# Six sums over partitions as two rounded products instead of one full-precision product

## The reference

```python
# state-space branch, after the gate: norm over 1024 channels
y = y.reshape(b, s, SSD_INNER) * jax.nn.silu(z.astype(jnp.float32))
return rmsnorm(y, norm_w).astype(z.dtype)
...
# retention branch: norm over the 256 channels of each of 4 heads
y = y * lax.rsqrt(jnp.mean(y * y, axis=-1, keepdims=True) + EPS)
y = y.reshape(b, s, RET_WIDTH) * jax.nn.silu(g.astype(jnp.float32))
...
# latent queries: norm over Q_LORA_RANK = 384 channels
c_q, q_mem = jnp.split(h @ w_in, [Q_LORA_RANK], axis=-1)
q = (rms_norm(c_q, g_q_lora) @ w_uq).reshape(b, s, MLA_HEADS, QK_HEAD_DIM)
```

## Time and profile before

| | |
|---|---|
| median of 3 runs | 2901.81 us (2900.05 to 2902.97) |
| the profiled execution | 2900.07 us, of which the span of the trace is 2898.2 us |
| granted TensorE clock | 1.0 of full speed, all through |
| TensorE busy | 2877.2 us |
| VectorE busy | 2192.0 us |
| ScalarE busy | 1383.4 us |
| GpSimd busy | 397.5 us |

### The profile page before, as it was taken

The page is one execution under the profiler, slowest core; times in us unless marked ns, Lnnn a source line. Parts: engine busy times, 40 slices in busy tenths (PEclk is TensorE's granted clock), DMA queues, the critical chain, the costliest instruction groups (busy, mean ns, idle before and its releaser), DMA issues.

```text
span 2898.2 us, 49038 instructions
## 1 busy us (share of the span) xinstructions
PE 2877.2 (99%) x17524; PEld 2531.7 (87%) x17524; DVE 2192.0 (76%) x3578; ACT 1383.4 (48%) x2252; POOL 397.5 (14%) x320
## 2 busy tenths in 40 slices
PE   9999999999999999999999999999999999999999
PEld 7888788778999888999887899989999887699987
DVE  8797574667999868888566888848889767688862
ACT  4653732344655525555233655525555236465541
POOL 0043250001111001110033011001110021011100
PEclk9999999999999999999999999999999999999999
DMA  3222123225577326773334477436773332257723
GB/s 139 102 92 91 66 95 116 73 80 179 160 183 180 89 95 181 181 180 103 107 109 132 129 180 180 117 114 179 184 182 106 107 111 74 83 155 184 182 80 109
DMA packets 144003, 375.93 MB, mean 130 GB/s; under 512 B 16176, under 2 KB 16432, under 8 KB 143472
## 3 DMA queue, kind: packets, MB, share of 16 engines
q1 hardware_dynamic: 110448, 309.44, 31.3%
q0 software_dynamic: 33408, 64.50, 13.0%
HBM read 371.78 MB, written 2.10 MB: 129 GB/s over the span
## 4 chain that ended last, share of the span: by engine, by line
PE 92%; DVE 5%; ACT 1%; issue 1%; DMA 0%; POOL 0%; SPq 0%; DVEq 0%; ACTq 0%; POOLq 0%
PE ps L1038 17%; PE ps L1040 17%; PE ps L1039 17%; PE ps L1492 12%; PE ps L1494 12%; PE ps L1493 12%; PE ps L1435 1%; DVE region_low L3594 0%; PE ps L1718 0%; PE ps L1755 0%; PE ps L1210 0%; DVE w_lo L2652 0%; DVE region_low L3222 0%; PE ps L1199 0%; PE ps L1424 0%
## 5 line engine op out<-in xcount | busy, mean ns | idle before, releaser
L1829 ACT ACTIVATE w_hi<-raw 128x1024 fp32r<-128x1024 f32 x300 | 315.8, 1055 | 281.4 <-DMA raw<-in_wstream 281.3
L1492 PE MATMUL ps<-h_hi,w_hi 128*128 128x256 f32 x1440 | 409.6, 284 | 1.6 <-DVE stage L3441 0.6
L1493 PE MATMUL ps<-h_lo,w_hi 128*128 128x256 f32 x1440 | 407.4, 283 | 0.0
L1038 PE MATMUL ps<-h_hi,w_hi 128*128 128x512 f32 (+1 forms) x883 | 347.4, 393 | 2.6 <-DVE w_lo L2652 1.8
L1040 PE MATMUL ps<-h_hi,w_lo 128*128 128x512 f32 (+1 forms) x883 | 340.7, 386 | 0.0
L1039 PE MATMUL ps<-h_lo,w_hi 128*128 128x512 f32 (+1 forms) x883 | 340.5, 386 | 0.0
L2652 DVE TENSOR_TENSOR w_lo<-raw,w_hi 128x1024 fp32r<-128x1024 f32 x220 | 265.8, 1220 | 80.7 <-ACT w_hi L1829 71.0
L1492 PEld LDWEIGHTS ps<-h_hi,w_hi 128*128 128x128 f32 x1440 | 276.0, 192 | 6.9 <-issue 2.6
L1493 PEld LDWEIGHTS ps<-h_lo,w_hi 128*128 128x128 f32 x1440 | 276.2, 192 | 0.4 <-issue 0.2
L942 POOL TENSOR_TENSOR w_lo<-raw,w_hi 128x1024 fp32r<-128x1024 f32 x78 | 195.9, 2515 | 494.3 <-ACT w_hi L1829 485.0
L1838 ACT ACTIVATE stage<-ps 128x512 f32<-128x512 f32 x107 | 63.6, 598 | 393.0 <-PE ps L1040 379.8
(11 more groups left out here) (694 smaller groups left out, 7634.1 us busy)
## 6 DMA issues: line engine op xcount, KB each, us to landing
raw<-in_wstream SPq DMA_DIRECT2D x300, 512.0 KB, 3.2
region<-in_pairs SPq DMA_DIRECT2D x193, 256.0 KB, 4.1
region<-in_pairs POOLq DMA_DIRECT2D x124, 256.0 KB, 5.5
region<-in_pairs SPq DMA_DIRECT2D x46, 512.0 KB, 5.7
last_pairs<-in_pairs SPq DMA_DIRECT2D x66, 256.0 KB, 4.0
raw<-in_pairs SPq DMA_DIRECT2D x22, 512.0 KB, 5.4
last_pairs<-in_pairs SPq DMA_DIRECT2D x22, 512.0 KB, 5.5
last_pairs<-in_pairs POOLq DMA_DIRECT2D x44, 256.0 KB, 5.6
```

Of the source, the lines that this page charges most:

```text
L1038: nc.tensor.matmul(dst, hi_w, hi_x, start=first, stop=False)
L1492: nc.tensor.matmul(dst, w1, x1, start=start, stop=False, skip_group_check=not first)
L1493: nc.tensor.matmul(dst, w1, x0, start=False, stop=False, skip_group_check=not first)
L1829: nc.scalar.activation(w_hi[:, n % HL], raw[:, r], ACT.Copy).then_inc(hi_ready, 1)
```

## The change

Six of the sums are made from two `fp32r` products instead of one `float32` product. VectorE rounds the sum of squares to `fp32r` in a spare tile of `tmp` (the high half) and subtracts it from `acc` in place (the low half). TensorE multiplies a matrix of ones by both, adding in PSUM. The ones are 8 rounded columns, `one_r`, of which one is read 128 times with a step of zero. `tmp_r` and `acc_r` are `fp32r` names for the same memory as `tmp` and `acc`. The other sums of the kernel stay as they are.

```diff
+        with ExitStack() as landing:
+            tmp_r = sb(landing, "tmp_r", [P, 4, S], F32R)
         tmp = sb(ctx, "tmp", [P, 4, S])
...
+        with ExitStack() as landing:
+            acc_r = sb(landing, "acc_r", [P, S], F32R)
         acc = sb(ctx, "acc", [P, S])
...
+        one_r = sb(ctx, "one_r", [P, 8], F32R)
...
+        ONES_R = one_r[:, 0:1].to_broadcast([P, P])
...
+            def two_sums(dst, hi, lo):
+                nc.tensor.matmul(dst, ONES_R, hi, start=True, stop=False)
+                return nc.tensor.matmul(dst, ONES_R, lo, start=False, stop=True)
+
+            def split_sum(value, hi, tiles):
+                pe.wait_ge(acc_ready, value)
+                if aux[0]:
+                    pe.wait_ge(aux_used, aux[0])
+                two_sums(ps[:, AUX], hi, acc_r[:]).then_inc(ss_done, 1)
+                norms[0] += 1
+                hs[0] += tiles
...
-                        norm_sum(posted, ST["z"].s + 8)
+                        split_sum(1, tmp_r[:, 2], DT)
...
-                norm_sum(acc_ready, 1 + hd, tiles=0)
+                split_sum(2 + hd, tmp_r[:, hd], 0)
...
-            memory_sum(5)
+            memory_sum(6)
...
-            latent_sum(tmp[:, 0], ONES, 3)
+            pe.wait_ge(sq_ready, 3)
+            two_sums(aux_tile(), tmp_r[:, 1], tmp_r[:, 0]).then_inc(aux_done, 1)
...
+            def two_halves(hi, lo, src):
+
+                done(v.tensor_copy(hi, src))
+                return v.tensor_tensor(lo, src, hi.bitcast(F32), ALU.subtract)
...
             v.tensor_copy(ident_r[:], mat["ident"])
+            v.tensor_copy(one_r[:], ONES[:, 0:8])
...
             gemm("z", gate_z, 2)
+            dve.wait_ge(posted, ST["z"].s + 8)
+            two_halves(tmp_r[:, 2], acc_r[:], acc[:]).then_inc(acc_ready, 1)
             reciprocal_root()
...
-                    square_sum(ret_out[hd % 2][j], acc_ready if j else None, scratch=spare[:, 0])
-                dve.wait_ge(acc_ready, hd + 1)
+                    square_sum(ret_out[hd % 2][j], None, scratch=spare[:, 0])
+                two_halves(tmp_r[:, hd], acc_r[:], acc[:]).then_inc(acc_ready, 1)
+                dve.wait_ge(acc_ready, hd + 2)
...
-                ins = v.tensor_tensor(tmp[:, 0], tmp[:, 0], tmp[:, k], ALU.add)
-                if k == 1:
-                    done(ins)
-            ins.then_inc(sq_ready, 1)
+                done(v.tensor_tensor(tmp[:, 0], tmp[:, 0], tmp[:, k], ALU.add))
+            two_halves(tmp_r[:, 1], tmp_r[:, 0], tmp[:, 0]).then_inc(sq_ready, 1)
```

## The result

The changed kernel takes 2906.43 us (median of 20 runs, 2904.5 to 2908.85) against 2901.19 us for the kernel before (20 runs). The ratio is 1.0019, with a 95% interval of 1.0013 to 1.0025: slower by 0.19%, or 5.2 us. I had forecast 2899.1 us with a range of 2896.5 to 2902.6, so the time lies outside the range and the change goes the other way. All times in this document are of undisturbed executions; one execution of `last_only64` took 3813.13 us at a mean granted clock of 0.692 and is left out.

A forecast was written before the change was run, and what follows sets the result against it. TensorE's queue was taken to bound the kernel, busy 2877.2 of 2898.2 us. Six sums save 2.7 us and VectorE's work costs nothing, so 2900.07 - 2.7 = 2897.3 us, median 2899.1 us, range 2896.5 to 2902.6.

The forecast's parts named there:

- What the sums cost and give: TensorE's queue at the six sums: each falls from 0.91 to 0.45 us, saving 2.7 us in all, bounds 0.5 and 2.7.
- What the work on VectorE costs: Copy and subtraction at each sum, about 1.15 us, 6.9 in all, costed at nothing because VectorE idles behind them.
- GpSimd beside the new pair: GpSimd splits near VectorE's copy and subtraction: could add up to 5.3 us; at the latent sum the pair fits GpSimd's pause.
- Rival (c): Latent queries: GpSimd holds up both VectorE operations, low half late, TensorE stands 2.8 us; 2901.9 us, chance 0.05.
- the sum, 2900.07 - 2.7: Whole kernel: 2897.3 us for an execution like the profiled one, so the median goes from 2901.81 to 2899.1 us.
- rival (e): Named the 32 bytes of one_r, tied to VectorE collisions with GpSimd; 6 us with either sign, chance 0.08.
- Rival (b): Six sums in TensorE's queue: step-zero ones run at full-precision pace, 0.91 us per product, adding 5.5 us; 2907.3 us, chance 0.04.

The follow-up runs named there:

- last_only64: Changed kernel with one_r behind small; only last half-product stage buffers from last_pairs on, spare, ident_r and small 64 bytes later: 2897.62 us.
- after_at_end: Changed kernel with one_r allocated behind small, the last buffer, so no buffer of the kernel before moves: 2898.27 us, ratio 0.9991.
- after_pad32: Changed kernel with 32 unused bytes behind one_r, so buffers behind it lie 64 bytes later than in the kernel before: 2892.48 us, ratio 0.9971.
- pad64: Kernel before with 64 unused bytes per partition behind neg_r, nothing else changed: 2895.47 us, ratio 0.998.
- pad32: Kernel before with 32 unused bytes per partition behind neg_r, no new instruction: 2909.06 us, ratio 1.0027.
- pad256: Kernel before with 256 unused bytes per partition behind neg_r, nothing else changed: 2899.5 us, ratio 0.9997.
- after_pad480: Changed kernel with 480 unused bytes behind one_r, so buffers behind it lie 512 bytes later than in the kernel before: 2899.79 us, ratio 0.9998.
- front64: Kernel before with 64 unused bytes in front of raw, the first buffer; all buffers move, distances kept: 2900.15 us, ratio 0.9998.
- behind_w64: Kernel before with 64 unused bytes behind w_hi; weight panels stay, h_hi, h_lo, x, tmp and all regions move: 2897.27 us, ratio 0.9991.
- round 4: Two placements of the changed kernel, one_r behind small: second allocation 64 bytes later, 2892.15 us; only last half-product stage's buffers 64 bytes later, 2897.62 us.
- after_pad96: Changed kernel with 96 unused bytes behind one_r, so buffers behind it lie 128 bytes later than in the kernel before: 2909.28 us, ratio 1.0027.
- after_pad160: Changed kernel with 160 unused bytes behind one_r, so buffers behind it lie 192 bytes later than in the kernel before: 2906.8 us, ratio 1.0022.

## Why the prediction was wrong, point by point

**What the sums cost and give.** Right. A sum took 0.91 us and takes 0.47 (predicted 0.45) at every shift, so six give back 2.6 us (predicted 2.7). By the measured times it is 2.3 us between after_at_end and the kernel before in the same round, with an interval that just touches no change, and 2.6 and 3.0 us between the kernels of equal shift at 32 bytes (2909.06 and 2906.43) and at 64 bytes (2895.47 and 2892.48).

**What the work on VectorE costs.** Right: nothing. A pair took 1.15 us and lay in idle time, and the low half of the latent queries was there 1.3 us before its sum started (1.4 forecast). The 7 us more of VectorE's busy time show where the placement is equal: 7.5 us in after_at_end (2199.5 against 2192.0), 7.2 in after_pad32 against pad64 (2197.2 and 2190.0), and 6.6 in the changed kernel against pad32 (2196.5 and 2189.9). At the start, the small copy took 0.16 us, hidden by idle time of 0.34.

**GpSimd beside the new pair.** Rival (c), in which GpSimd holds up both operations of VectorE, did not come about. At the latent sum the pair fell into GpSimd's pause: it ran from 2380.43 to 2381.58, and GpSimd was idle from 2379.12 to 2382.12. At the state-space sum it did not quite: the subtraction runs from 407.49 to 408.18, and a split of GpSimd starts inside it.

```profile
407.94 2.50 POOL L948 TENSOR_TENSOR w_lo<-raw,w_hi 128x1024 fp32r<-128x1024 f32 x1 [1.49 <-ACT w_hi L1848]
412.07 2.41 POOL L948 TENSOR_TENSOR w_lo<-raw,w_hi 128x1024 fp32r<-128x1024 f32 x1 [1.64 <-ACT w_hi L1848]
```

The subtraction keeps its 0.69 us, and the split, which came later, takes 0.1 us more than the next one. It had no effect on the time there: TensorE is busy for all of the 260.00 us from 400 to 660. The same overlap is in the traces of all eight kernels that have the change: the subtraction takes 0.69 us, the split that starts inside it 2.50 to 2.51 and the next one 2.39 to 2.41.

**The step that failed** is the sum, 2900.07 - 2.7: it gave `one_r` no term for where it was put, and costed it as one small copy. With it fell a premise that I had not written out, that an ordinary product costs 0.227 us wherever its operands lie. The 512-column products on moved buffers went to 234 ns: 3879 of them, 24.0 us. The half products gained 13.9 us. With the 0.5 us of `gated_x_low` that makes 10.6 us of loss; the traces differ by 8.5 us, and what is missing, 2.1 us, is near the gain of the sums. (The medians differ by 5.2 us, the two profiled executions by 8.5.) My rival (e) named the 32 bytes, but tied them to collisions of VectorE with GpSimd, and gave them 0.08 with either sign. No run shows that the placement moves such collisions, or the 6 us that I had put on them: VectorE's panel splits keep their mean of 1.22 us, and pad32, which has none of the new work, loses 8.1 us. Nor does another engine set the pace: of the products on `br`, `mg`, `region_low` and `gated_a_low`, 245 in the trace of before and 236 in that of pad32 run while VectorE, ScalarE and GpSimd stand still and no DMA packet moves, and they too go from 226.7 to 233.3 ns on the mean. Rival (b), which named 2907.3 us, was wrong in spite of the near number: the products with ones of step zero take 0.235 us and not 0.91.

**What is shown and what is not.** Shown: the loss follows the shift without the work (pad32), the work without the shift gains (after_at_end), shifts of 256 and 512 bytes leave 227 and 120 ns as they were (pad256, after_pad480), it hangs on the distance between buffers and not on their starts (front64, behind_w64), and it is there without any other engine at work. Not shown: why. The weight load of a product starts together with the product before it (both at 561.80 in the earlier trace rows), and both operands are SBUF buffers of `kernel.py`. That these two reads get in each other's way at some distances is my guess; no run separated them. One row speaks against the guess as the whole story. Neither `gated_x_low` nor its weights `w_hi`, nor the panel loaded next, moved in the shifts of the regions, and yet its 128 products went from a median of 227 ns to 231 (shift 32), 229 (64), 226 (128) and 237 (192). What did move are the operands of the neighbouring products, such as `last_pairs_low`. So the distance from the weights is not the only one that counts, and which pairs of operands matter stays open. Other engines are not needed for the effect, by the 226.7 and 233.3 ns above. If the two reads never meet, my guess is wrong, and something else makes the difference of 2909.06 to 2895.47 us with identical instructions; no run here tells. It also stays open why the half products are fastest at 64 and 192 bytes and the wide ones at 0, and whether one placement could have both. The best rows of the two columns, -16.5 and -2.7 us, would together be 19 us below the kernel before, where after_pad32 has 9; the two attempts of round 4 did not get nearer.

## What to carry to other kernels

In these kernels allocating a buffer moved every buffer behind it, and 32 bytes of it alone changed the time by 0.3% (pad32). When TensorE is the bound, compare the start-to-start distance of equal products before and after, by the buffer that they read, before you look for waits. Test an edit with its new buffers put last, so that no other buffer moves, and try a few pads of 32 to 192 bytes as a tuning step of its own: here it was worth from -0.2% (pad64) to +0.3% (pad32), more than the 0.1% of the edit. And take a product's price from a trace with the same placement: the one that I had read as 227 ns was 226 to 237 ns under the shifts tried here.

## What the runs showed of the hardware that I had not expected

- The pace of `fp32r` products at full clock went with how far apart within a partition the buffers lie that TensorE reads: with all of them moved by 64 bytes it stayed at 227 ns (front64), with `h_hi` moved by 64 against the weights its products went from 227 to 230 (behind_w64), and at shifts of 256 and 512 bytes the regions had their 227 again (pad256, after_pad480). By the shift of the regions against the weight panels, medians of all products on the regions with 512 columns: 227 ns at 0, 234 at 32 (pad32), 229 at 64 (pad64; 226 to 234 by operand), 232 at 128 (after_pad96) and 233 at 192 (after_pad160). Half products: 120 ns at 0 and 118 at the four others.
- The records of the weight loads of the half products differ too: a mean of 192 ns before and 188 ns in the changed kernel, for the same form. Their rows before and after:

```profile
L1492 PEld LDWEIGHTS ps<-h_hi,w_hi 128*128 128x128 f32 x1440 | 276.0, 192 | 6.9 <-issue 2.6
```

```profile
L1510 PEld LDWEIGHTS ps<-h_hi,w_hi 128*128 128x128 f32 x1440 | 271.0, 188 | 6.6 <-issue 2.8
```

- A weight matrix read as one column with step zero is loaded in 188 ns (187 to 188 for the twelve loads of lines 1134 and 1135 in the changed kernel), as the blocks of `w_lo` are (median of 188 at line 1040 before), and the load is hidden under the product before it: the two products of a sum start 234 to 235 ns apart.
